# Moving 20 of 80 modulation columns, and three landing buffers in place of four, in a two-layer hybrid backbone step

## What is computed

```python
mp = (jax.nn.silu(c_ctx) @ ada_w[i] + ada_b[i]).reshape(6, D_MODEL)       # prompt
ms = (jax.nn.silu(c) @ ada_w[i] + ada_b[i]).reshape(-1, 6, 1, D_MODEL)    # sample
hp = xp * (1.0 + mp[1]) + mp[0]                                            # shift, scale of the mixer
...
xp = _layer_norm(ALPHA * xp + mp[2] * yp, ln_w[i, 0], ln_b[i, 0])          # gate of the mixer
fp = _hier_moe(xp * (1.0 + mp[4]) + mp[3], *wm)                            # shift, scale of the experts
xp = _layer_norm(ALPHA * xp + mp[5] * fp, ln_w[i, 1], ln_b[i, 1])          # gate of the experts
```

## Time and profile before

| | |
|---|---|
| median of 3 runs | 1387.97 us (1385.61 to 1388.39) |
| the profiled execution | 1388.39 us, its span 1386.6 us, 1.8 us around it |
| PE busy | 1209.8 us (87%) |
| DVE busy | 721.8 us (52%) |
| ACT, POOL busy | 343.8 us (25%), 209.5 us (15%) |
| granted TensorE clock, mean | 0.936 |
| chain that ended last, by engine | PE 61%, DVE 12%, DMA 12%, issue 9%, ACT 4%, SP's queue 1% |
| DMA | 290.17 MB, mean 209 GB/s |
| L1906, all 160 instructions | 137.2 us + 44.1 us by the two largest groups |

### The profile page before, as it was taken

The page is one execution under the profiler, slowest core; times in us unless marked ns, Lnnn a source line. Parts: engine busy times, 40 slices in busy tenths (PEclk is TensorE's granted clock), DMA queues, the critical chain, the costliest instruction groups (busy, mean ns, idle before and its releaser), DMA issues.

```text
span 1386.6 us, 14689 instructions
## 1 busy us (share of the span) xinstructions
PE 1209.8 (87%) x5174; PEld 657.2 (47%) x5174; DVE 721.8 (52%) x1578; ACT 343.8 (25%) x728; POOL 209.5 (15%) x305
## 2 busy tenths in 40 slices
PE   5998887999999799799575999989998998899573
PEld 2555454554456444644222555656666443743221
DVE  0499345442277787541013475558886777541014
ACT  1422231222310010311013242334555211311011
POOL 5012210000011110002201401003334110003101
PEclk9999897999999999899797999999999899799797
DMA  9553000227398575299945332234435697399943
GB/s 376 201 207 139 1 1 30 107 107 257 117 366 318 199 290 227 108 407 422 420 160 205 137 132 68 99 107 150 138 127 184 207 380 296 133 418 418 421 155 139
DMA packets 75844, 290.17 MB, mean 209 GB/s; under 512 B 7692, under 2 KB 18188, under 8 KB 61436
## 3 DMA queue, kind: packets, MB, share of 16 engines
q1 hardware_dynamic: 41952, 191.12, 35.6%
q0 software_dynamic: 16352, 60.44, 11.8%
q10 hardware_dynamic: 17468, 37.67, 7.4%
HBM read 261.30 MB, written 27.90 MB: 209 GB/s over the span
## 4 chain that ended last, share of the span: by engine, by line
PE 61%; DVE 12%; DMA 12%; issue 9%; ACT 4%; SPq 1%; POOL 0%; ACTq 0%; POOLq 0%; DVEq 0%
PE bank L580 13%; PE bank L600 11%; PE bank L739 7%; DMA arena<-in_moe_gu 4%; PE bank L948 4%; PE bank L759 3%; DVE arena L1930 3%; PE bank L1135 3%; DMA ring<-in_ada_w 3%; DVE arena L1906 2%; DVE arena L2484 2%; PE bank L839 2%; DMA ring<-in_b_w_out 1%; PE bank L881 1%; PE bank L976 1%
## 5 line engine op out<-in xcount | busy, mean ns | idle before, releaser
L580 PE MATMUL bank<-hT,ring 128*128 128x384 f32 x896 | 299.3, 495 | 4.8 <-ACT hT L1520 1.7
L580 PEld LDWEIGHTS bank<-hT,ring 128*128 128x128 f32 x896 | 172.2, 194 | 124.3 <-issue 8.2
L600 PE MATMUL bank<-ring,arena 128*128 128x512 f32 (+1 forms) x512 | 176.1, 609 | 10.8 <-DVE arena L2096 7.3
L1906 DVE SCALAR_TENSOR_TENSOR arena<-arena 128x1024 f32<-128x1024 f32 x112 | 137.2, 1225 | 11.8 <-DMA arena<-in_ada_wT 9.1
L739 PE MATMUL bank<-arena,hT 128*64 128x512 f32 x416 | 106.0, 629 | 36.0 <-DMA arena<-in_moe_gu 25.0
L600 PEld LDWEIGHTS bank<-ring,arena 128*128 128x128 f32 (+1 forms) x512 | 72.9, 196 | 104.3 <-issue 86.8
L1930 DVE SCALAR_TENSOR_TENSOR arena<-arena,par 128x388 f32<-128x388 f32 x160 | 100.0, 625 | 5.7
L1135 PE MATMUL bank<-hT,ring 128*128 128x384 f32 x256 | 96.3, 501 | 0.2 <-ACT arena L1534 0.2
L739 PEld LDWEIGHTS bank<-arena,hT 128*64 128x64 f32 x416 | 37.1, 144 | 93.2 <-issue 87.6
L1376 POOL DMA_DIRECT2D arena<-in_ada_wT x74 | 39.1, 529 | 263.2 <-DVE arena L1906 256.9
L1465 POOL TENSOR_TENSOR arena<-arena 128x192 f32<-128x192 f32 x64 | 43.1, 703 | 217.0 <-PE bank L1168 158.4
(11 more groups left out here) (422 smaller groups left out, 1645.1 us busy)
## 6 DMA issues: line engine op xcount, KB each, us to landing
arena<-in_moe_gu SPq DMA_DIRECT2D x56, 1024.0 KB, 27.2
arena<-in_ada_wT POOLq DMA_DIRECT2D x74, 512.0 KB, 5.9
arena<-in_moe_dn SPq DMA_DIRECT2D x28, 1024.0 KB, 13.2
ring<-in_b_w_in SPq DMA_DIRECT2D x40, 512.0 KB, 3.5
ring<-in_a_w_in SPq DMA_DIRECT2D x32, 512.0 KB, 6.4
ring<-in_moe_gu SPq DMA_DIRECT2D x12, 1024.0 KB, 13.8
arena<-acs_rows ACTq DMA_DIRECT2D x32, 384.0 KB, 3.5
yg<-arena ACTq DMA_DIRECT2D x18, 512.0 KB, 8.3
```

What stands on the lines that cost most here:

```text
L580: last = mm(keys[j][1][:, 0:T], w[:, k, P * j:P * j + P], hT[:, 4 * half + k, :], start=half == 0 and k == 0, stop=half == 1 and k == 3, s ...
L600: last = mm(keys[t][1][p:p + tokens.shape[1], :], tokens, w[:, j, :], start=k == 0, stop=k == KE - 1, skip_group_check=True)
L1906: ins = ve.scalar_tensor_tensor(out=products, in0=c_slots[place][i % 4], scalar=1.0, in1=rows[:, v, :], op0=ALU.mult, op1=ALU.mult, accum_ ...
```

## The change

The 80 columns get four places and three landing buffers each: 12, 20, 24 and 24 columns. In place 0 the columns stand after convolutions 1 to 12, one each. Place 1 has its 20 in the loop over the heads, two each in the first ten chunks, and none ahead of it. A new place 2 lies in memory that is free once the last head is transposed (`hT` and the old rows), and its 24 columns stand after the diagonals. Place 3 is the old place 2; its columns stand as 6, diagonals, eviction, 18. The total of columns is the same.

```diff
-        gone_at, far_at = KE * T + 4 * D, ARENA - 7 * D
...
-        c_slots = [[free(o + D * i) for i in range(4)] for o in (q_at + 3 * D, far_at)]
-        c_slots.append([free(gone_at), free(gone_at + D), hT_free[:, 2 * D:3 * D], free(ARENA - 12 * MSLAB)])
-        COLUMNS = (16, 40, 24)
+        gone_at, far_at = KE * T + 4 * D, ARENA - 6 * D
...
+        c_slots = [[free(o + D * i) for i in range(3)] for o in (q_at + 3 * D, far_at)]
+        c_slots += [[free(gone_at), free(gone_at + D), hT_free[:, 2 * D:3 * D]]] * 2
+        COLUMNS = (12, 20, 24, 24)
@@ weights in SP's order
-            if s == 0:
-                prefetch(0, 4)
-            elif 4 <= s < 7:
-                prefetch(0, 5 + s)
-        for m in range(5, 9):
-            prefetch(0, m)
+            prefetch(0, 4 + s)
...
-            if 6 <= s < 15:
+            if s >= 6:
                 prefetch(1, s - 6)
-        for m in (10, 11, 9):
+        for m in range(10, STATIC):
@@ their waits
-                elif l == 1 and m == 9:
-                    sp.wait_ge(sem("summed"), sum(COLUMNS))
-                elif l == 0 and m == 5:
+                elif l == 0 and m == 6:
                     sp.wait_ge(sem("summed"), sum(COLUMNS[0:2]))
@@ columns on POOL
-                    if i >= 4:
-                        pool.wait_ge(sem("summed"), i - 3)
-                    if place == 1 and i % 4 == 0:
-                        pool.wait_ge(sem("out_mn"), 32)
-                    pool.dma_start(c_slots[place][i % 4], i_["ada_wT"][l, j]).then_inc(column_landed(i)[0], 16)
+                    if i >= 3:
+                        pool.wait_ge(sem("summed"), i - 2)
+                    pool.dma_start(c_slots[place][i % 3], i_["ada_wT"][l, j]).then_inc(column_landed(i)[0], 16)
...
             columns(1)
+            pool.wait_ge(filled, group["hn", KE - 1][1])
+            columns(2)
             moe(0)
@@ ACT
-            c_silu(1)
...
                 ac(a_sz[:, c, :], ps[:, 0:T], ACT.Silu).then_inc(read("in"), 1)
+                if c == 0:
+                    c_silu(1)
+            c_silu(2)
@@ DVE: after convolution c
-                if c < KE - 1:
-                    summed(0, 2 if c == 6 else 1)
-            biased(0, 16, 32)
+                if 1 <= c < 13:
+                    summed(0, 1)
+            biased(0, 16, 28)
@@ ahead of and in the loop over the heads
-            summed(1, 4)
...
-                summed(1, 2 if c % 4 == 3 else 1)
+                if c < 10:
+                    summed(1, 2)
+            biased(0, 28, 48)
@@ before mixed(0, "yA")
             diagonals(0)
-            summed(1, 16)
-            biased(0, 32, 48)
+            summed(2, 24)
             biased(1, 0, 24)
@@ before mixed(2, "yB")
             diagonals(2, (0, 1))
-            summed(2, 12)
+            summed(3, 6)
             diagonals(2, (2, 3))
-            summed(2, 2)
             ps = await_bank(dve, "single", 4)
             ve.tensor_scalar(rms, ps[:, 0:NT], float(D) / E2, EPS, ALU.mult, ALU.add).then_inc(read("single"), 1)
-            summed(2, 10)
+            summed(3, 18)
```

More of the change, by code:

```diff
@@ L201, in program @@
         q_at = KE * T + KE * W_PAD
-        gone_at, far_at = KE * T + 4 * D, ARENA - 7 * D
-        c_rows = [v3(a, 2) for a in (free(q_at, 2 * D), free(far_at + 5 * D, 2 * D), hT_free[:, 0:2 * D])]
-        c_products = (free(q_at + 2 * D), free(far_at + 4 * D), free(KE * T + 2 * D))
-        c_slots = [[free(o + D * i) for i in range(4)] for o in (q_at + 3 * D, far_at)]
-        c_slots.append([free(gone_at), free(gone_at + D), hT_free[:, 2 * D:3 * D], free(ARENA - 12 * MSLAB)])
-        COLUMNS = (16, 40, 24)
+        gone_at, far_at = KE * T + 4 * D, ARENA - 6 * D
+        c_rows = [v3(a, 2) for a in (free(q_at, 2 * D), free(far_at + 4 * D, 2 * D), hT_free[:, 0:2 * D], hT_free[:, 0:2 * D])]
+        c_products = (free(q_at + 2 * D), free(far_at + 3 * D), free(KE * T + 2 * D), free(KE * T + 2 * D))
+        c_slots = [[free(o + D * i) for i in range(3)] for o in (q_at + 3 * D, far_at)]
+        c_slots += [[free(gone_at), free(gone_at + D), hT_free[:, 2 * D:3 * D]]] * 2
+        COLUMNS = (12, 20, 24, 24)
         column_of = [(place, l, j) for place, (l, j) in zip(
-            [p for p in range(3) for _ in range(COLUMNS[p])], [divmod(2 * KD + i, 48) for i in range(80)])]
-        COLUMN_SEMS = ("pool_in0", "pool_in1", "pool_in2", "xc_in0")
+            [p for p in range(4) for _ in range(COLUMNS[p])], [divmod(2 * KD + i, 48) for i in range(80)])]
         def column_landed(i):
-            moe = (32, 32, 32, 16 * (NPAIR // 2 - 1))[i % 4] if i >= sum(COLUMNS[0:2]) else 0
-            return sem(COLUMN_SEMS[i % 4]), 16 * (i // 4 + 1) + moe
-        def columns_in(l, j):
-            return 16 * len(range(j, sum(COLUMNS[0:2 + l]), 4))
+            return sem(f"pool_in{i % 3}"), 16 * (i // 3 + 1) + (32 if i >= sum(COLUMNS[0:3]) else 0)
         def rows_landed(l, t):
-            return sem(f"pool_in{t}"), 32 * (l + 1) + columns_in(l, t)
+            n = sum(COLUMNS) if l else sum(COLUMNS[0:3])
+            return sem(f"pool_in{t}"), 32 * (l + 1) + 16 * len(range(t, n, 3))
         nrow = e_r[0:32, 0:P]
@@ L720, in turn_tokens @@
                 def turn_tokens(q):
-                    n = 16 * ((NPAIR // 2 - 1 + q % 2) * l + q // 2 + q % 2)
-                    pe.wait_ge(sem(f"xc_in{q % 2}"), n if q % 2 else n + columns_in(l, 3))
+                    pe.wait_ge(sem(f"xc_in{q % 2}"), 16 * ((NPAIR // 2 - 1 + q % 2) * l + q // 2 + q % 2))
                     for stage, k0 in (("txA", 0), ("txB", 4)):
@@ L1486, in _ @@
             pool.wait_ge(filled, group["in", 3 * KE - 1][1])
-            columns(2)
+            columns(3)
             moe(1)
@@ L1844, in _ @@
             z_silu(12, 15)
-            c_silu(2)
+            c_silu(3)
             new_state(6)
@@ L1905, in summed @@
                     for v in range(2):
-                        ins = ve.scalar_tensor_tensor(out=products, in0=c_slots[place][i % 4], scalar=1.0, in1=rows[:, v, :],
+                        ins = ve.scalar_tensor_tensor(out=products, in0=c_slots[place][i % 3], scalar=1.0, in1=rows[:, v, :],
                                                       op0=ALU.mult, op1=ALU.mult, accum_out=mod[:, l, j, v:v + 1])
```

## The result

The kernel after takes 1429.85 us in the median of 4 runs (1428.35 to 1433.28), the kernel before 1387.18 beside it (1385.61 to 1388.39). The ratio is 1.031, with a 95% interval of 1.029 to 1.033. The forecast of 1407 us had the direction right and less than half of the size; the time lies outside its range. The two traces differ by 44.7 us of span (1431.3 against 1386.6), and the prediction is measured against that.

The account below looks back on a forecast made before the run. PE was taken to bound the kernel, with 61% of the chain of waits. The sum -12.5 + 10.6 + 21.0 = +19.1 us on 1388.4 gave 1407.5, less 0.4 by the median: 1407 us, range 1394 to 1425.

Parts of the forecast that it names:

- PE's wait near 134 us: Behind the convolutions: PE's wait for ACT was to be gone after the change.
- Part A: Convolutions, place 0: four of 16 columns leave, PE resumes 10.4 us earlier and slow-clock matmuls go; 12.5 us gained.
- a stretch in which DVE never idles: Convolutions, place 0: four columns of 2.54 us taken out of DVE's unbroken work save 10.2 us.
- Part B: Layer 0, places 1 and 2: DVE's added columns and landing waits delay the first norm's last transpose; 10.6 us lost.
- The projection back starts at 466 in place of 470.0: End of layer 0's loop over heads: chunk 13 is emptied at once, so the next stage starts earlier.
- Part C: Layer 1, place 3: 18 columns remain behind the eviction where 10 did, with long landings; 21.0 us lost.
- With 25 us to the last transpose: Second norm: from `mixed` at 1184.3 this long to the last transpose, at 1209.3 where it was 1188.3.
- the end of SP's backlog: Layer 1, place 3: SP's 16.5 MB of expert pieces and slabs end near 1164, with 10.5 of 18 columns done.
- Edits at nothing: Third SiLU, row DMA, earlier z slabs, SP's prefetches and POOL's expert work: each set at no effect on the time.
- landings stay long: Rival, places 2 and 3: ten microseconds per landing in place 3, one more in place 2; 1434 us, chance 0.12.
- Landings shrink with the load: Rival, places 2 and 3: with two in flight landings fall under 4.7 us, three buffers suffice; 1387 us, chance 0.07.
- PE ends both norms: Rival, both norms: DVE has slack enough for the added columns, so the change is faster; 1371 us, chance 0.05.

Follow-up runs that it names:

- the best version: Kernel before with 12 columns among convolutions, none in the last four chunks, 5 between layer 0's diagonals, layer 1's slabs ahead of expert pieces, 5 unread matmuls: 1364.06 us.

## Why the prediction was wrong, step by step

The mechanism it named for the loss is the one that acts: DVE becomes the bound at both norms, and PE idles there. Four signs came as told: no column waits in place 0 for its landing, DVE idles near 18 us ahead of the diagonals (19.8), columns wait for their landings in places 2 and 3 (11.5 and 14.0 us), and PE waits at both norms. Three did not: PE's wait near 134 us is not gone (4.09), q, k and v do not start at 1.46 us (2.07), and the projection back starts 7.0 us earlier and not some 16. The three parts of the sum were all too favourable, by 6.5, 9.2 and 9.2 us; with 0.7 from the stretches set at nothing that makes the 25.6 us between 19.1 and 44.7.

- **Part A, -12.5 forecast, -6.0 in the trace.** The step that failed is "PE's own work reaches to 133 to 134, so it hardly idles, and the 1.2 GHz stretch behind the idle time should go". PE's work reached to 133.3, as told, but the last convolution ended at 135.5, not 132.7, so PE idled 4.09 us and resumed at 137.34, not 134.6. The clock still fell to 0.66, and the way to the z projection took 229.0 us where it took 227.3 before and where the forecast took 2.1 off. That is 2.7 + 3.8 of the 6.5 us. Filling the idle time brings that way to 223.6 us: this part of the gain exists, but only without the pause. The late convolution goes back to "a stretch in which DVE never idles". Without a column behind convolution 0, DVE is ready for convolution 2 too early and waits 1.88 us. The profile names no engine that ended this wait, but ACT copies a chunk from 64.41 to 64.97 us, having waited 5.78 us for PE:

```profile
65.06 0.42 DVE L1916 TENSOR_SCALAR arena<-arena,par 128x388 f32<-128x388 f32 x1 [1.88 <-issue]
```

- **Part B, +10.6 forecast, +19.8.** "The projection back starts at 466 in place of 470.0" was to win 4 us in the loop over the heads; it won 1.0, because two columns in each of ten chunks made DVE late in the chunks between, where PE waited 2.6 and 1.9 us, and 2.1 at the end. I had counted PE's wait at the end of the loop and not the ones inside. From the start of the projection back to place 2 it took 18.1 us, as forecast. Then 73.2 us to `mixed`, where I had 70 (waits of 11.5, not 9). From `mixed` to the last transpose it took 27.5 us, not 24.5. That is 3.0 + 3.2 + 3.0 us. The last of these was too short already by the kernel before: from the first transposes on the sum has 14 us, that kernel takes 16.6, and the kernel after 17.4.
- **Part C, +21.0 forecast, +30.2.** From the first diagonals to `mixed` 106.4 us, where my step had 101.4: the 18 columns took 59.4 us for 55.6, at 8.3 to 9.7 us a landing beside SP's backlog, near the 8.5 expected, but for longer, and they began 1.3 us later. From `mixed` to the last transpose 29.2 us where I took 25. The 25 us came from a norm in which PE is busy; in one in which PE has waited 29 us, its first transposes take 1.97 us instead of 1.09 and the 16 products behind them 5.76 instead of 3.71, at a granted clock of 0.61 and not 0.98. These two groups are 2.9 of the 4.2 us; the runs leave open how much of the rest is the clock. So two steps failed here: "With 25 us to the last transpose", short by 4.2 us, and the end of SP's backlog, which the forecast has 81 us behind the first diagonals (1164 - 1083) and the trace, by the landings, about 87 (1183 - 1096), so that the 18 columns took 3.8 us more.
- **Edits at nothing** hold: between the norms the traces differ by 0.3 us, behind the second by 1.0.

The rival "landings stay long" gave 1434 us, near the result, but by another road: it had A at its full 12.5, C at 39, and landings of ten microseconds whatever is in flight. Its B of 19.7 meets the 19.8 by luck, for it puts `mixed` 79 us behind the start of place 2, where 73.2 were measured. The trace refutes its mechanism, since landings were 3.7 us again behind SP's backlog, and so do the runs in which SP's pieces were held back. "Landings shrink with the load" is right in its direction and wrong in its size: with at most one other column in flight they were 8.1 to 8.2 us in place of 9.6 to 11.1, still far above the 4.8 us at which it decides. What brings them below that is SP's load, which the change left in place. "PE ends both norms" is refuted by the waits of 21.9 and 29.2 us.

Of the change's three edits, the order is the largest: 20 us for layer 1 alone. Another 14 us come with five columns put between the diagonals of layer 0, which mends that stage and is not the old order. Giving up the fourth buffer costs 12 us behind the new order, and 3 in the kernel before. The edit that was to win, four columns out of place 0, wins 1 to 5 us.

## What to carry to other kernels

When work moves on an engine that another engine waits for later, look first for that engine's own idle time ahead of the move: a piece of work put behind a wait instead of into it costs its full length once the slack there is used up, and one landing buffer less then costs 12 us instead of 3. Add up a chain with the durations of the state that the change brings about (in layer 1 the stretch from the first transposes to the last took 15.2 us with a busy PE and 18.9 behind a wait), and test the sum on the trace that you have: the one for layer 0 was 2.5 us short there already. And where two queues share the DMAs, what sets a landing is above all the backlog of the other queue, so moving its transfers is an edit of its own, worth 10 to 16 us here.

## What was not expected of the hardware

- A pause of PE costs something beyond its length, and a longer one need not cost more. With 4.1 us of idle time filled by five matmuls that nobody reads, the 229.0 us behind it became 223.6 (and 228.2 became 224.5 in the best version, which fell from 1371.49 to 1364.06 us in all); behind an idle time of 7.2 to 7.4 us it was 227.3 to 228.4. Where PE waited 3.75 us inside the loop over the heads (the run with the old order in layer 1) the next 32 matmuls took 13.48 us; after a wait of 1.90 us in the kernel after they took 10.59.
- The place of a slow stretch moves between traces of kernels whose PE does the same work up to there: eight matmuls near 190 us took 5.28, 4.44 or 2.74 us, while the way from where PE resumes to the z projection stayed at 228 to 230 us. A single slow group is poor evidence for a cause; a stretch between two fixed events is better.
- A 512 KB landing took 3.7 us in a quiet stretch and 8.4 to 9.1 in the 42 us in which another queue moved 12.8 MB at 416 GB/s in all. With two or three others of its own queue in flight besides it was up to 11.1.
